# A decoder block on one core: x handed over transposed, weights tile by tile, one chunk of columns per head, attention over three chunks

## The reference

```python
h = rmsnorm(x, g_norm)                 # x * rsqrt(mean(x^2) + eps) * g
z = h @ w_in                           # 2048 -> 12296 columns
qa, ka, va, ga, qb, kb, vb, gb, fl, ma, mb = split(z)   # 8 x 1024, 8, 2 x 2048
# branch A, 8 heads: rope on the first 16 of each 64, two softmax maps per head
a = softmax(q0 k0 / 8, causal) - lam * softmax(q1 k1 / 8, causal)
oa = rmsnorm(a @ va, g_subln) * (1 - lam_init) * silu(ga)
# branch B, 8 heads of 128
c = cumsum(log_sigmoid(fl + b_forget))
ob = softmax(qb kb / sqrt(128) + c_i - c_j, causal) @ vb * silu(gb)
m = sigmoid(ma) * (oa @ w_proj_a) + sigmoid(mb) * (ob @ w_proj_b)
y = rmsnorm(x + m @ w_out, g_final)
```

## Time and profile before

| | us |
|---|---|
| runs | 777.76, 778.96, 780.96 |
| median of the runs | 778.96 |
| span of the profiled execution, first to last instruction | 775.0 |
| median less span: what lies around it | 3.96 |
| TensorE busy in the profiled execution | 759.5 |
| VectorE, ScalarE, GpSimd busy | 432.2, 370.1, 72.2 |

### The profile page before, as it was taken

One profiled execution on the slowest core, in us unless ns is written; L12 is line 12 of the kernel. 1 busy time (PEld: TensorE's weight loads), 2 busy tenths in 40 slices (PEclk: granted clock), 3 DMA queues, 4 the chain that ended last, 5 costly groups with the idle time before them and its releaser, 6 DMA issues.

```text
span 775.0 us, 11206 instructions
## 1 busy us (share of the span) xinstructions
PE 759.5 (98%) x3592; PEld 629.2 (81%) x3592; DVE 432.2 (56%) x632; ACT 370.1 (48%) x552; POOL 72.2 (9%) x97
## 2 busy tenths in 40 slices
PE   5999999999999999999999999999999999999996
PEld 4888888888888888888888888888888888888886
DVE  3655444454555555554765666656665665665562
ACT  3654444444454445544455545545555544444441
POOL 3010000010011101112600000000000000001110
PEclk9999999999999999999999999999999999999999
DMA  9758676766666565666655656566555655855542
GB/s 224 225 174 257 197 195 189 191 192 190 186 169 182 166 181 170 170 181 167 184 154 173 173 165 177 162 166 185 163 163 172 201 195 181 339 186 192 197 153 109
DMA packets 73621, 143.34 MB, mean 185 GB/s; under 512 B 4568, under 2 KB 6640, under 8 KB 73088
## 3 DMA queue, kind: packets, MB, share of 16 engines
q1 hardware_dynamic: 72800, 140.79, 61.4%
q0 software_dynamic: 480, 1.48, 1.0%
q10 hardware_dynamic: 320, 0.79, 0.3%
HBM read 140.94 MB, written 2.11 MB: 185 GB/s over the span
## 4 chain that ended last, share of the span: by engine, by line
PE 96%; DMA 2%; issue 1%; SPq 0%; DVE 0%; ACT 0%; DVEq 0%; POOLq 0%; POOL 0%
PE Z L254 29%; PE Z L256 29%; PE Z L255 29%; PE Z L354 3%; DMA diff_z<-in_x 2%; PE A L318 1%; PE A L294 1%; PE Dk L311 1%; PE B L303 1%; PE A L369 0%; PE Dk L325 0%; PE B L333 0%; PE A L333 0%; PE C L303 0%; PE C L286 0%
## 5 line engine op out<-in xcount | busy, mean ns | idle before, releaser
L679 DVE TENSOR_TENSOR w_lo<-w_raw,w_hi 128x1024 fp32r<-128x1024 f32 x248 | 306.7, 1239 | 233.3 <-ACT w_hi L478 231.1
L478 ACT ACTIVATE w_hi<-w_raw 128x1024 fp32r<-128x1024 f32 x244 | 258.0, 1058 | 233.3 <-PE Z L256 230.2
L254 PE MATMUL Z<-w_hi,hT_hi 128*128 128x512 f32 (+1 forms) x848 | 336.8, 397 | 0.0
L256 PE MATMUL Z<-w_hi,hT_lo 128*128 128x512 f32 (+1 forms) x848 | 330.2, 389 | 0.0
L255 PE MATMUL Z<-w_lo,hT_hi 128*128 128x512 f32 (+1 forms) x848 | 329.6, 389 | 0.0
L256 PEld LDWEIGHTS Z<-w_hi,hT_lo 128*128 128x128 f32 x848 | 159.2, 188 | 34.2
L254 PEld LDWEIGHTS Z<-w_hi,hT_hi 128*128 128x128 f32 x848 | 159.4, 188 | 31.6 <-issue 0.2
L255 PEld LDWEIGHTS Z<-w_lo,hT_hi 128*128 128x128 f32 x848 | 159.5, 188 | 30.3
L254 PE MATMUL Z<-w_hi,oT_hi 128*128 128x512 f32 x128 | 50.2, 392 | 0.0
L256 PE MATMUL Z<-w_hi,oT_lo 128*128 128x512 f32 x128 | 49.8, 389 | 0.0
L255 PE MATMUL Z<-w_lo,oT_hi 128*128 128x512 f32 x128 | 49.8, 389 | 0.0
(11 more groups left out here) (196 smaller groups left out, 544.5 us busy)
## 6 DMA issues: line engine op xcount, KB each, us to landing
w_raw<-in_w_in SPq DMA_DIRECT2D x192, 512.0 KB, 3.8
w_raw<-in_w_out SPq DMA_DIRECT2D x32, 512.0 KB, 4.1
w_raw<-in_w_a SPq DMA_DIRECT2D x16, 512.0 KB, 3.7
w_raw<-in_w_b SPq DMA_DIRECT2D x16, 512.0 KB, 3.7
diff_z<-in_x SPq DMA_DIRECT2D x8, 256.0 KB, 10.6
diff_z<-in_x SPq DMA_DIRECT2D x1, 2048.0 KB, 8.7
rows<-c_rows_dram POOLq DMA_DIRECT2D x1, 1024.0 KB, 6.4
rows<-in_g_final SPq DMA_DIRECT2D x1, 1024.0 KB, 10.7
```

Of the source, the lines that this page charges most:

```text
L254: pe.matmul(acc, a_hi, b_hi, start=first, stop=False)
L256: return pe.matmul(acc, a_lo, b_hi, start=False, stop=last)
L478: act.activation(w_hi[:, j % RING], w_raw[:, j % RING], ACT.Copy).then_inc(hi_ready, 1)
L679: dve.tensor_tensor(w_lo[:, j % RING], w_raw[:, j % RING], w_hi[:, j % RING].bitcast(fp32), ALU.subtract).then_inc(lo_ready, 1)
```

## The change

Host side, x is also handed over transposed (`xT`, 128 x 16 x 256), g_norm as a column block, and all small inputs in one block of constants with the identity matrix. All weights are laid out so that each tile is one contiguous block with 4 KB for a partition (`laid_out`). The columns of w_in are reordered so that chunk c holds q, k, v and gate of head c (128 columns each), forgetting heads first.

Chunk 1 is special: it is cut in two halves of 4 tiles, each of 4 k-blocks. The first has q and k of head 1 and the 8 forget-gate columns (`FL_COLS` = 264 columns), the second v and gate of head 1 (256 columns). So the forget logits come out of PSUM bank Z with q and k, and `wfl` and its products are gone.

The mean of squares: ScalarE squares `xT` in 8 operations between the splits of tiles 8 to 11, VectorE sums over the 16 k-blocks (`x_ssq`), and TensorE sums over the partitions by a product with ones after the first tile of chunk 1; VectorE, GpSimd and VectorE make `rstd` of it.

Attention: head h is spread over chunks h+2 to h+4, in two bursts for a chunk, after tile 1 and after tile 5. In a chunk c three heads are in work. Heads read q, k, v and gate in a ring of three chunk buffers `z_sb` (`head_copy` is gone), rope is done by GpSimd per head (12 small operations), and both score blocks are split products. The merge gates are made by `tanh` straight from PSUM. The loops are written out.

```diff
             for t in range(TILES):
+                sp.dma_start(xT_sb[:, 2 * t:2 * t + 2, :], xT[:, 2 * t:2 * t + 2, :]).then_inc(x_loaded[t], 16)
+                if t == 0:
+                    sp.dma_start(w_raw[:, 0, 0:CHUNK], w_main[0][:, 0:CHUNK]).then_inc(first_half, 16)
+                    sp.dma_start(w_raw[:, 0, CHUNK:2 * CHUNK], w_main[0][:, CHUNK:2 * CHUNK]).then_inc(raw_loaded[0], 16)
+                else:
+                    load(t)
...
+                    S = (B, C)[i]
+                    split_product(S[:, 0:P], qkT_hi[part, 0:P], qkT_lo[part, 0:P],
+                                  qkT_hi[part, 2 * P:3 * P], qkT_lo[part, 2 * P:3 * P], True, True)
+                    mm = split_product(S[:, P:3 * P], qkT_hi[part, P:2 * P], qkT_lo[part, P:2 * P],
+                                       qkT_hi[part, 2 * P:4 * P], qkT_lo[part, 2 * P:4 * P], True, True)
...
+            def attention(c, j):
+                if j == 1:
+                    if 0 <= c - 4 < N_HEADS:
+                        gated_transposes(c - 4)
+                    if 0 <= c - 3 < N_HEADS:
+                        prob_transposes(c - 3)
+                    if 0 <= c - 2 < N_HEADS:
+                        head_transposes(c - 2)
+                if j == 5:
+                    if 0 <= c - 3 < N_HEADS:
+                        values(c - 3)
+                    if 0 <= c - 2 < N_HEADS:
+                        scores(c - 2)
+
+            pe.wait_ge(warm_ready, 1)
+            for _ in range(3):
+                pe.matmul(Dk[:, 0:3 * P], warm[:, 0:P], warm[:], start=True, stop=True)
...
+            for j in range(4):
+                tile(8 + j, 1, hT_hi, hT_lo, 4 * j, 4, FL_COLS, j == 0, j == 3)
+                if j == 0:
+                    pe.wait_ge(x_summed, 1)
+                    pe.wait_ge(consts_loaded, 16)
                     for m in range(M_TILES):
+                        mm = pe.matmul(A[:, m:m + 1], x_ssq[:, m * P:(m + 1) * P], ones[:, 0:1], start=True, stop=True)
+                    mm.then_inc(ms_done, 1)
+            banks_free(2)
+            for j in range(4):
+                tile(12 + j, 0, hT_hi, hT_lo, 4 * j, 4, 2 * HD, j == 0, j == 3)
...
             for j in range(TILES):
+                act.activation(x_sq[:, 2 * j:2 * j + 2, :], xT_sb[:, 2 * j:2 * j + 2, :], ACT.Square,
+                               scale=D_MODEL ** -0.5).then_inc(x_squared, 1)
                 if j < 4:
+                    split(8 + j)
+
+            act.wait_ge(rstd_ready, 1)
+            evacuate(0)
+            split(12)
+            act.wait_ge(w_used, 12)
+            act.wait_ge(fl_ready, 1)
+            act.activation(z_sb[:, 1, 0, 0:2 * HD], Z[2][:, 0:2 * HD], ACT.Copy, scale=rstd[:, 0:1]).then_inc(evac[0], 1)
+            split(13)
...
+            for j in range(3):
+                split(8 + j)
+            dve.wait_ge(x_squared, 8)
+            dve.tensor_reduce(x_ssq[:], x_sq.rearrange("p k n -> p n k"), AX.X, ALU.add).then_inc(x_summed, 1)
+            split(11)
+            dve.wait_ge(ms_done, 1)
...
+                    if j == 7 and 0 <= c - 2 < N_HEADS:
+                        normalizers(c - 2)
+                        if c - 2 >= HEADS:
+                            combine_maps(c - 2)
...
             pool.memset(neg_half[:], -0.5).then_inc(pool_const, 1)
+            pool.wait_ge(hi_ready, 5)
+            pool.dma_start(consts[:], consts_in).then_inc(consts_loaded, 16)
```

More of the change, by code:

```diff
@@ L143, in build @@
[L143 to L160, removed]
@@ new lines, in _ @@
+            for t in range(TILES):
+                sp.dma_start(xT_sb[:, 2 * t:2 * t + 2, :], xT[:, 2 * t:2 * t + 2, :]).then_inc(x_loaded[t], 16)
[4 more added lines that the diff above has]
+                    load(t)
+            for t in range(TILES, 8 * OUT):
+                load(t)
@@ new lines, in _ @@
+            act.wait_ge(act_step, 2)
+            act.activation(fl_abs[:], fl_abs[:], ACT.Ln, bias=1.0).then_inc(softplus_ready, 1)
+            split(14)
+            act.wait_ge(lam_dots, 2)
+            act.activation(lam_exp[:], lam_dot[:], ACT.Exp).then_inc(lam_exps, 1)
+            split(15)
+            for t in range(16, 20):
+                split(t)
+            act.wait_ge(w_used, 16)
+            act.activation(z_sb[:, 1, 0, 2 * HD:4 * HD], Z[0][:, 0:2 * HD], ACT.Copy, scale=rstd[:, 0:1]).then_inc(evac[0], 1)
@@ new lines, in _ @@
+            act.wait_ge(half_ready, 1)
+            for c in range(2, PROJ):
+                for j in range(TILES):
+                    split(8 * c + j + RING)
+                    if j == 1:
+                        if 0 <= c - 4 < N_HEADS:
+                            gated_hi(c - 4)
+                        if 0 <= c - 3 < N_HEADS:
+                            head_pT(c - 3)
+                        if 0 <= c - 2 < N_HEADS:
+                            head_qkT(c - 2)
+                    if j == 2 and 0 <= c - 3 < N_HEADS:
+                        tanh(c - 3)
+                    if j == 5 and HEADS <= c - 3 < N_HEADS:
+                        out_square(c - 3)
+                    if j == 6 and 0 <= c - 2 < N_HEADS:
+                        exps(c - 2)
+                if c < MERGE:
+                    evacuate(c)
+                else:
+                    if c == MERGE:
+                        act.wait_ge(evac[1], fill_of(MERGE))
+                    merge_tanh(c)
@@ L674, in chained, with counted, split @@
                 dve.wait_ge(dve_step, step[0])
-            def split(c, j):
-                dve.wait_ge(hi_ready, 8 * c + (j + 5))
-                dve.tensor_tensor(w_lo[:, j % RING], w_raw[:, j % RING], w_hi[:, j % RING].bitcast(fp32),
+            def counted(ins):
+                step[0] += 1
+                ins.then_inc(dve_step, 1)
+                return step[0]
+            def split(t):
+                dve.wait_ge(hi_ready, t + 1)
+                n = width(t)
+                dve.tensor_tensor(w_lo[:, t % RING, 0:n], w_raw[:, t % RING, 0:n], w_hi[:, t % RING, 0:n].bitcast(fp32),
@@ new lines, in _ @@
+            evacuate(0)
+            split(12)
+            dve.wait_ge(w_used, 12)
+            for m in range(M_TILES):
+                ins = dve.scalar_tensor_tensor(fl[:, m, :], Z[2 + m][:, 2 * HD:FL_COLS], rstd[:, m:m + 1], b_row,
+                                               ALU.mult, ALU.add)
+            ins.then_inc(fl_ready, 1)
+            dve.tensor_scalar(z_sb[:, 1, 1, 0:2 * HD], Z[3][:, 0:2 * HD], rstd[:, 1:2], None, ALU.mult).then_inc(evac[1], 1)
+            split(13)
+            for i in range(2):
+                dve.tensor_tensor_reduce(lam_tmp[:, i], lam_in[:, 2 * i, :], lam_in[:, 2 * i + 1, :], 1.0, 0.0,
+                                         ALU.mult, ALU.add, lam_dot[:, i:i + 1]).then_inc(lam_dots, 1)
@@ L1039, in _ @@
+            for c in range(2, PROJ):
+                if 0 <= c - 2 < HEADS:
+                    head_bias(c - 2)
+                if HEADS <= c - 1 < N_HEADS:
+                    rope(c - 1)
+                if HEADS <= c - 3 < N_HEADS:
+                    pool.wait_ge(o_ms_ready, c - 3 - HEADS + 1)
+                    pool.tensor_tensor(o_rstd[:], o_ms[:], neg_half[:], ALU.pow).then_inc(o_rstd_ready, 1)
             pool.wait_ge(gf_loaded, 16)
```

997 lines of the change are left out of this document (419 added, 578 removed).

## The result

The changed kernel takes 785.61 us (median of 4 runs, 784.66 to 788.1) against 778.38 us for the kernel before beside it (777.76 to 780.96): a ratio of 1.0101, 95% interval 1.0077 to 1.0125. The forecast was 773.5 with a range of 768.5 to 780. The profiled execution has a span of 784.0 us against 775.0. These are 9.0 apart and the medians 7.2: in every run with both on record the time lies some 1.8 us above its own span, so the profiled execution before (775.0 + 1.8) was about 2 us quicker than the median.

What follows compares the result with a forecast made beforehand. The prediction took TensorE's matmuls as the bound, after a start where TensorE needs earlier feeding. Span: 775.0 - 9.9 (chunk 0) + 3.8 (chunk 1) + 0.6 (attention) = 769.5 us; with 3.96 from span to median, 773.5, range 768.5 to 780.

## What to carry to other kernels

Where TensorE is the bound and its operands come from a ring, keep the slot's size a multiple of 256 bytes (shown here for 512-column products), and look at the starts of products by slot, since a busy share of 100% hides a longer pitch. Make a statistic that the engines wait for while its input streams in, and lay out the values that VectorE sums by what both sides pay. Hold back small strided or broadcast DMAs until the first large loads are in.

## What the hardware showed that I had not expected

- A 512-column product whose moving operand begins 128 bytes off a multiple of 256 starts 0.2326 to 0.2333 us after the one before it in place of 0.2267, 2.6 to 2.9%. With slots at 64, 128 and 192 bytes off, a tile of 12 took 2.76, 2.79 and 2.80 in place of 2.72. 256-column products showed no such cost (0.1187 to 0.1189 off, 0.1193 to 0.1201 on). After slow tiles, the first three products of an aligned one are slow as well (0.231 to 0.2325).
- TensorE ran at 1.2 GHz for 10.2 us around and behind one idle of 7.4 us (6.8 us in the kernel with 4352-byte slots, with the same idle), and at 2.4 GHz over the same stretch when 6.6 us of it were filled.
- VectorE's sum of 4096 values took 7.0 us at a stride of 1 KB (7.5 in the two runs with the early squares) and 4.42 side by side; ScalarE wrote 512 squares 64 bytes apart in about 0.92 us and side by side in 0.54.
- Eight small DMAs of GpSimd of 0.4 MB in all cost the first chunk 4.2 us in the traces; put out later, they left the whole kernel 6.0 us shorter by the medians.
